# Six layers of two transformer stacks on one core: token halves taken in turn at the borders between phases, turned heads in a score bank, weight steps in quarters

## The reference

```
x = x + 0.5 * swiglu(rms_norm(x, ffn1_norm[l]), ffn1_w13[l], ffn1_w2[l])
h = rms_norm(x, mix_norm[l]);  three attention branches (differential, sliding with sinks, latent)
x = x + jnp.sum(gates * proj, axis=2) @ w_out[l]
x = x + 0.5 * swiglu(rms_norm(x, ffn2_norm[l]), ffn2_w13[l], ffn2_w2[l])
```

```
x = x + 0.5 * rms_norm_2(swiglu_2(rms_norm_2(x, g[0]), ffn_w_in[i, 0], ffn_w_out[i, 0]), g[1])
m = sliding_sink / nsa / moba / sliding_sink attention of rms_norm_2(x, g[2])     (i = 0, 1, 2, 3)
x = x + rms_norm_2(m, g[3])
x = x + 0.5 * rms_norm_2(swiglu_2(rms_norm_2(x, g[4]), ffn_w_in[i, 1], ffn_w_out[i, 1]), g[5])
```

## Time and profile before

| | |
|---|---|
| median of 3 runs | 3773.41 us (3771.87 to 3777.15) |
| the profiled execution | 3778.8 us, span 3777.0 us |
| PE busy | 3436.2 us, 91% of the span |
| PEld, DVE, ACT, POOL busy | 78%, 58%, 48%, 2% |
| mean granted TensorE clock | 0.926 of full speed |
| HBM | 615.62 MB read, 166 GB/s over the span |

### The profile page before, as it was taken

One profiled execution on the slowest core, in us unless ns is written; L12 is line 12 of the kernel. 1 busy time (PEld: TensorE's weight loads), 2 busy tenths in 40 slices (PEclk: granted clock), 3 DMA queues, 4 the chain that ended last, 5 costly groups with the idle time before them and its releaser, 6 DMA issues.

```text
span 3777.0 us, 49507 instructions
## 1 busy us (share of the span) xinstructions
PE 3436.2 (91%) x18184; PEld 2940.8 (78%) x18184; DVE 2186.5 (58%) x2330; ACT 1803.9 (48%) x2261; POOL 92.5 (2%) x208
## 2 busy tenths in 40 slices
PE   7987899999779899998899998789999989998799
PEld 6876677878677788787787877678787978787687
DVE  5565465555655555556555565555656655556555
ACT  4454444444554454445444453344445544444444
POOL 0000000000000000000000000100000000000000
PEclk9987899999878999998999996679999999999899
DMA  6653345545433455454354543235454444454254
GB/s 236 218 188 112 109 169 181 181 178 189 145 106 120 153 189 189 176 180 148 142 179 177 189 167 123 72 106 189 178 191 178 161 150 178 176 191 168 100 200 167
DMA packets 105050, 618.45 MB, mean 164 GB/s; under 512 B 10816, under 2 KB 19008, under 8 KB 34656
## 3 DMA queue, kind: packets, MB, share of 16 engines
q1 hardware_dynamic: 84288, 562.07, 41.4%
q10 hardware_dynamic: 20640, 54.71, 4.3%
HBM read 615.62 MB, written 9.50 MB: 166 GB/s over the span
## 4 chain that ended last, share of the span: by engine, by line
PE 83%; DVE 7%; ACT 4%; issue 3%; DVEq 1%; POOL 1%; DMA 0%; ACTq 0%; POOLq 0%
PE ps L1520 32%; PE ps L1524 16%; PE ps L1584 6%; PE ps L1583 6%; PE ps L1585 6%; PE ps L1541 2%; PE ps L1542 2%; PE ps L1543 2%; PE ps L1559 2%; PE ps L1683 1%; PE ps L1672 1%; DVE wlo L985 1%; ACT v L633 1%; PE ps L1697 1%; PE ps L1698 1%
## 5 line engine op out<-in xcount | busy, mean ns | idle before, releaser
L1520 PE MATMUL ps<-xhl,whi 128*128 128x512 f32 x4944 | 1734.7, 401 | 34.8 <-DVEq L401 34.8
L985 DVE TENSOR_TENSOR wlo<-raw,whi 128x2048 fp32r<-128x2048 f32 x526 | 1204.1, 2292 | 784.4 <-ACT whi L597 784.3
L1524 PE MATMUL ps<-xhl,wlo 128*128 128x256 f32 x4944 | 1289.6, 281 | 0.0
L597 ACT CAST whi<-raw 128x2048 fp32r<-128x2048 f32 x526 | 999.8, 1904 | 226.5 <-PE ps L1585 128.0
L1520 PEld LDWEIGHTS ps<-xhl,whi 128*128 128x128 f32 x4944 | 905.4, 190 | 217.2 <-issue 41.8
L1524 PEld LDWEIGHTS ps<-xhl,wlo 128*128 128x128 f32 x4944 | 946.6, 191 | 55.4
L1584 PE MATMUL ps<-wlo,ht 128*128 128x512 f32 x1056 | 417.2, 395 | 0.0
L1583 PE MATMUL ps<-whi,ht 128*128 128x512 f32 x1056 | 417.1, 395 | 0.0
L1585 PE MATMUL ps<-whi,ht 128*128 128x512 f32 x1056 | 416.6, 395 | 0.0
L670 ACT COPY tg<-ps 128x512 f32<-128x512 f32 x132 | 77.5, 587 | 430.9 <-PE ps L1520 430.9
L1585 PEld LDWEIGHTS ps<-whi,ht 128*128 128x128 f32 x1056 | 198.3, 188 | 48.1
(11 more groups left out here) (242 smaller groups left out, 3718.1 us busy)
## 6 DMA issues: line engine op xcount, KB each, us to landing
raw<-stream SPq DMA_DIRECT2D x528, 1024.0 KB, 4.8
bias<-rel_bias ACTq DMA_DIRECT2D x80, 256.0 KB, 2.7
gain<-gains ACTq DMA_DIRECT2D x19, 1024.0 KB, 4.7
bias<-fixed_bias ACTq DMA_DIRECT2D x40, 256.0 KB, 2.6
rel_bias<-rel_vectors SPq DMA_DIRECT2D x16, 512.0 KB
x<-x_tokens ACTq DMA_DIRECT2D x1, 1024.0 KB, 4.8
y_tokens<-x ACTq DMA_DIRECT2D x1, 1024.0 KB, 3.9
cst<-constants ACTq DMA_DIRECT2D x1, 670.0 KB, 6.6
```

The costliest lines, as they stand in the source:

```text
L597: nc.scalar.copy(whi[:, slot, :], raw[:, slot, :]).then_inc(sem["hi_ready"], 1)
L985: nc.vector.tensor_tensor(wlo[:, slot, :], raw[:, slot, :], whi[:, slot, :].bitcast(F32), ALU.subtract).then_inc(sem["lo_ready"], 1)
L1520: wide = lambda: pe.matmul(ps[:, bank, 0:2 * half], hi[:, k, col0:col0 + P], src[:, k0 + k, :], start=first and k == 0, stop=last and k == ...
L1524: e = pe.matmul(ps[:, bank, 0:half], lo[:, k, col0:col0 + P], src[:, k0 + k, 0:half], start=False, stop=False)
```

## The change

Borders: the whole chain of a between runs for token half 0 and then for half 1, on ScalarE, GpSimd and VectorE, and the splits of the next phase's steps 1 and 2, which stood behind it, are put inside it. PE has no between any more: the next phase turns a half itself (`arrive`), waits for its low parts (`arrived`, new semaphore `x_low`) and multiplies half 0 of its first two steps, turning half 1 in the middle. For that these products are token-major (96 matmuls of 256 columns in an ffn in place of 32 of 512 and 32 of 256). In an ffn the first pair's SwiGLU is then taken token-major by halves and turned by four PE transposes into bank 6. In a projection with such a lead, v comes first; the stream of weights is laid out in that order. gqa2's first group needs both halves at once. At the end of an ffn the last two down steps are done for half 0 and then for half 1; in the plain output projection (`wout`) the last two steps as well.

Weaves: turned heads go to the score bank of the next slot in place of bank 3; the values no longer wait for their low parts, the scores of the next slot do. `brw` has four buffers for two. Product steps are issued in quarters, the tables name how many per slot: gqa2 2, 2, eleven times 1, four times 2, 1, 0; moba twelve times 3, six times 2, 0. Groups of moba come as v, q, k for q, k, v.

```diff
@@ slots
-GQA_SLOTS = {0: [(2, 0)], 1: [(2, 1)], 2: [(3, 0)], 4: [(3, 1)], 5: [(4, 0)], 7: [(4, 1)], 9: [(5, 0)],
...
+GQA_SLOTS = slots_of([part for j in range(2, 8) for part in quarters(j)],
+                     [2, 2] + [1] * 11 + [2, 2, 2, 2, 1, 0])
+MOBA_SLOTS = slots_of([part for j in range(3, 15) for part in quarters(j)],
+                      [3] * 12 + [2] * 6 + [0])
@@ plan, second stack: order of the groups
-        project(f("q", 0, 2), f("k", 0, 2), t("v", 0, 512, 4, 2, 1))
+        project(t("v", 0, 512, 4, 2, 1), f("q", 0, 2), f("k", 0, 2))
...
-            project(f("k", 0, 1), t("v", 0, 256, 8, 1, 1), f("k", 4, 1), t("v", 256, 256, 8, 1, 1),
-                    t("gate", 0, 48, 8, 1, 1))
+            project(f("k", 0, 1), f("k", 4, 1), t("gate", 0, 48, 8, 1, 1))
...
-            by_four = [g for n in range(4) for g in f("q", 4 * n, 1) + f("k", 4 * n, 1) + t("v", 256 * n, 256, 8, 1, 1)]
+            by_four = [g for n in range(4) for g in t("v", 256 * n, 256, 8, 1, 1) + f("q", 4 * n, 1) + f("k", 4 * n, 1)]
@@ ScalarE, ffn and weave
+                def first_pair(tt):
+
+                    if tt == 0:
+                        act.wait_ge(sem["ag_made"], base(ph, "ag_made") + 1)
+                    else:
+                        multiplied(ph.step + 1)
+                    nc.scalar.activation(silu[:, tt, :], ps[:, 4 + tt, 0:T], ACT.Silu).then_inc(sem["silu_first"], 1)
...
+                first_pair(0)
                 split(ph.step + 3)
+                first_pair(1)
+                act.wait_ge(sem["tposed"], base(ph, "tposed") + 1)
+                nc.scalar.copy(ht[:, 0, :, 0, :], ps[:, 6, :].rearrange("p (k t) -> p k t", k=2))\
+                    .then_inc(sem["hi_made"], 1)
...
-                def turned(k):
+                def turned(k, bank):
                     act.wait_ge(sem["tposed"], B["tposed"] + k + 1)
-                    if k >= 4:
-
-                        multiplied(ph.step + n_g + k // 2 - 2)
-                    nc.scalar.copy(brw[:, k // 2 % 2, k % 2, 0:T], ps[:, 3, T:2 * T]).then_inc(sem["hi_made"], 1)
@@ VectorE, between
+                step = after_of(ph).step
+                if ph.gains == 0:
+
+                    dve.wait_ge(sem["vec_stored"], 16)
+                if ph.after == "post":
+                    gained(0)
+                added(0)
+                if ph.final:
+                    final_norm(0)
+                normed(0)
+                if ph.after == "post":
+                    gained(1)
+                else:
+                    added(1)
                 if ph.gains == 0:
                     split(0)
+                low_parts_of(0)
+                if ph.after == "post":
+                    added(1)
+                if ph.final:
+                    final_norm(1)
+                split(step + 1)
+                normed(1)
+                low_parts_of(1)
+                split(step + 2)
@@ TensorE: arrival of a token half, ffn, project, weave
+            def arrive(ph, tt):
+
+                last = before_of(ph)
+                pe.wait_ge(sem["xn_ready"], base(last, "xn_ready") + tt + 1)
+                for half in range(2):
+                    n, k0 = 2 * tt + half, 4 * half
                     for k in range(4):
                         e = pe.transpose(ps[:, n, k * P:(k + 1) * P], o[:, tt, (k0 + k) * P:(k0 + k + 1) * P], ident)
                     e.then_inc(sem["tposed"], 1)
+
+            def arrived(ph, tt):
+
+                last = before_of(ph)
+                pe.wait_ge(sem["x_low"], base(last, "x_low") + 2 * tt + 2)
+
+            def token_cols(dst, w, col0, width, src, tt, ks=range(KD), k0=0, first=0, last=KD - 1):
+
+                hi, lo = (part[:, :, col0:col0 + width] for part in w)
+                for k in ks:
+                    xh = src[:, k0 + k, tt * P:(tt + 1) * P]
+                    xl = src[:, k0 + k, T + tt * P:T + (tt + 1) * P]
+                    pe.matmul(dst, xh, hi[:, k, :], start=k0 + k == first, stop=False)
+                    pe.matmul(dst, xh, lo[:, k, :], start=False, stop=False)
+                    e = pe.matmul(dst, xl, hi[:, k, :], start=False, stop=k0 + k == last)
...
+                def first_pair(tt, turn_between):
+
+                    for part in range(2):
+                        use(ph.step + part)
+                        w = step_parts(ph.step + part, KD, 2 * P)
+                        dst = ps[:, 4 + tt, part * T:(part + 1) * T]
+                        token_cols(dst, w, 0, 2 * P, xhl, tt, range(KD // 2))
+                        if turn_between and part == 1:
+                            arrive(ph, 1)
+                        e = token_cols(dst, w, 0, 2 * P, xhl, tt, range(KD // 2, KD))
+                        if tt == 1:
+                            e.then_inc(sem["step_used"], 1)
+                    if tt == 0:
+                        e.then_inc(sem["ag_made"], 1)
+
+                arrive(ph, 0)
+                arrived(ph, 0)
+                first_pair(0, True)
+                arrived(ph, 1)
+                first_pair(1, False)
+                use(ph.step + 2)
+                w = step_parts(ph.step + 2, KD, 2 * P)
+                feature_tile(0, w, 0, xhl)
+                for tt in range(TT):
+                    pe.wait_ge(sem["h_first"], base(ph, "h_first") + tt + 1)
+                    for kk in range(2):
+                        e = pe.transpose(ps[:, 6, kk * T + tt * P:kk * T + (tt + 1) * P],
+                                         h[:, tt, kk * P:(kk + 1) * P], ident)
+                e.then_inc(sem["tposed"], 1)
+                feature_tile(1, w, P, xhl).then_inc(sem["step_used"], 1)
+                pe.wait_ge(sem["ht_first"], base(ph, "ht_first") + 1)
+                down(ph.step + 3, first=True)
+                up(ph.step + 4, 2)
                 with pe.Fori(2, PAIRS - 1) as j:
                     body(j, ph.step - 1, j)
...
+                for tt in range(TT):
+                    for i in range(2):
+                        c = end - 2 + i
+                        if tt == 0:
+                            pe.wait_ge(sem["ht_ready"], base(ph, "ht_ready") + last - 1 + i)
+                            use(c)
+                        w = step_parts(c, 2, D)
+                        for kk in range(2):
+                            e = rows_by(w, i, tt, kk, False, i == 1)
+                        if tt == 1:
+                            e.then_inc(sem["step_used"], 1)
+                    if tt == 0:
+                        e.then_inc(sem["acc_half"], 1)
...
+                    k = weave_turn(t - 1)
+                    if k is not None:
+
+                        pe.wait_ge(sem["lo_made"], B["lo_made"] + k + 1)
...
-                def turn_heads(k):
+                def turn_heads(k, bank):
                     pe.wait_ge(sem["o_done"], B["o_done"] + 2 * k + 2)
+                    pe.wait_ge(sem["biased"], B["biased"] + min(2 * k + 4, ph.n))
                     for tt in range(TT):
-                        e = pe.transpose(ps[:, 3, T + tt * P:T + (tt + 1) * P], o[:, tt, k * P:(k + 1) * P], ident)
+                        e = pe.transpose(ps[:, bank, tt * P:(tt + 1) * P], o[:, tt, k * P:(k + 1) * P], ident)
                     e.then_inc(sem["tposed"], 1)
 
...
+                arrive(ph, 0)
+                if ph.groups[0].dest != "v":
+                    arrive(ph, 1)
+                    arrived(ph, 1)
+                arrived(ph, 0)
+                for quarter in range(4 * ph.early):
+                    if ph.groups[0].dest == "v" and quarter == 1:
+                        arrive(ph, 1)
+                    if quarter == 2:
+                        arrived(ph, 1)
+                    product(quarter // 4, quarter % 4)
                 for t in range(ph.n + 3):
...
-                    if here:
-                        part_of(*here[0])
+                        turn_heads(k, (t + 1) % 2)
+                    first = (len(here) + 1) // 2
+                    for part in here[:first]:
+                        part_of(*part)
                     if 1 <= t <= ph.n:
                         turn_probs(t - 1)
-                    if len(here) > 1:
-                        part_of(*here[1])
+                    for part in here[first:]:
+                        part_of(*part)
                     if 2 <= t <= ph.n + 1:
@@ TensorE, wout
-                for i in range(4):
+                for i, tt in ((0, 0), (0, 1), (1, 0), (1, 1), (2, 0), (3, 0), (2, 1), (3, 1)):
```

402 lines of the change are left out of this document (220 added, 182 removed), and 3 rows, old and new, of the table MOBA_SLOTS.

## The result

The changed kernel takes 3783.41 us (median of 20 runs, 3771.66 to 3789.90), the kernel before on the same chip 3774.84 (20 runs): ratio 1.0028, 95% interval 1.0021 to 1.0036. I had forecast 3750.5 us, faster; it is 8.6 us slower by the medians, 10.6 by the ratio. The profiled executions differ by 4.4 us (span 3781.4 against 3777.0).

A forecast was written before the change was run, and what follows sets the result against it. TensorE's work plus its standing, mostly at borders, was taken to bound the kernel. Terms 15.8 + 12.2 - 11.9 - 1.2 + 20 - 12 = 22.9 us, off a median of 3773.41, gave 3750.5 us; range 3728 to 3778.

The forecast's parts named there:

- What bounds it: Whole kernel: TensorE's work plus its standing still; the largest wait, 94.8 us, is for normed tokens at the borders.
- plain borders: Borders behind a phase without output norm: both first steps done at 16.1 us, gain 3.2 us behind an FFN.
- the end of an FFN: Last two down steps, now by token halves: TensorE stands about 1.2 us for `ht` in each of 12 FFNs.
- Post borders behind FFNs: Borders behind FFNs with normed output, into FFNs: both first steps done at 19.8 us, gain 1.9 us at three.
- Behind weaves and the final norm: Borders into FFNs there: gain 0.6 us at each of three behind weaves, 3.8 us at the final norm.
- clock* rival: Every border, moba and gqa2: products fall into the half clock, 37.6 us lost, 3788 us; chance 0.12.
- Borders before gqa2: Both borders into gqa2: its first group needs both halves, so nothing covers half 1; loss 4.8 us, twice.
- The first attention's stop: Layers 0 and 1 of the first stack: attention waits for the last k, 10.1 us for 5.16 now.
- covered by the gate step alone: NSA: second k's low parts, 9.3 us behind its matmuls, are covered only by about 5.6 us: -3.7.
- Gain 10 us, twice: Both gqa2 weaves: quarters give every slot product, leaving 4 us of stops; 10 us gained in each.
- nothing from the quarters: Rival for gqa2's weaves: VectorE's queue sets the slots, the 20 us go, 3770.5 us; chance 0.15.
- 5.3 + 3 x 4.6: moba's weave: scores wait for k's emptying, 5.3 us once and 4.6 three times; new stops 19.2 us, loss 12.

The follow-up runs named there:

- e5: Changed kernel with moba's groups v first once, then k, q, v, plus spare TensorE work filling stops before FFNs: 3743.13 us, ratio 0.9918 to the kernel before.
- e7: Changed kernel with moba's groups v first once, then k, q, v, plus another VectorE and ScalarE order at borders before gqa2: 3750.30 us, ratio 0.9930.
- e1: Changed kernel with moba's groups back in the order q, k, v: 3758.77 us, ratio 0.9960 to the kernel before.
- e3: Changed kernel with the old slot tables (half products) in both weaves, new bank and group order kept: 3777.20 us, ratio 1.0006 to the kernel before.
- e8: Changed kernel with moba v first once, then k, q, v, plus VectorE's weight split in gqa2 cut to 128 of 2048 columns: 3730.54 us, ratio 0.9890.
- e10: Changed kernel with turned heads in bank 3 again, quarters and group order kept: 3787.18 us, ratio 1.0026 to the kernel before.
- e4: Changed kernel with everything inside the weaves as before (slots, bank, moba's q, k, v), borders new: 3767.03 us, ratio 0.9978 to the kernel before.
- e13: Changed kernel with moba v first once, then k, q, v, plus ScalarE's weight split in gqa2 cut to 128 of 2048 columns: 3746.48 us, ratio 0.9925.
- e14: Changed kernel with moba v first once, then k, q, v, plus VectorE's emptying and weight split later in all weaves' slots: 3744.79 us, ratio 0.9925.
- e6: Changed kernel with moba v first once, then k, q, v, plus the last two down steps of each FFN mixed: 3756.38 us, ratio 0.9950.

## Why the prediction was wrong, by its steps

- **What bounds it, plain borders, the end of an FFN: right.** Both steps are done 15.86 us after E (forecast 16.1), the gain is 3.3 us (3.2), and the stop is 1.03 us (1.2) in each FFN. The product there ran at a granted clock of 1.00 from its start; before, it was 0.88 over the same work.
- **Post borders behind FFNs: right in the mark.** Done at 20.05 us (19.8), though some 4 us of the product run at half clock, which is more than my 0.3 us of slack has room for; e5 shows that most of it was covered. Behind weaves and the final norm: mechanism right, sizes off. Done at 23.5 and 24.5 us, where I had 22.0 and 20.6 (the 26.2 of before less 3.8, 0.55 and 1.2), and 5.2 to 5.8 us of the product run at half clock. The *clock* rival named this for every border; it came at the post ones and the final norm alone, and its sign, a mean clock below 0.926, did not come (0.931). Removing it in e5 returned 0.9 us behind an FFN and 1.4 to 1.8 behind a weave, as much as the weave borders missed (1.5); at the final norm e5 didn't remove it, and that miss of 3.9 us stays open.
- **Borders before gqa2: right.** First products at 14.4 and 13.8 us (13.7), the first scores 5.5 and 3.1 us later than before (4.8 forecast for each), and e7 took 3 us of the loss back with the order I had blamed. The first attention's stop is 10.03 us (10.1).
- **NSA, the second k "covered by the gate step alone": not settled.** 285.1 us is 2.3 us better than forecast, but the same code took 284.9 to 285.3 us in eight of the profiled executions and 287.8 to 288.9 in four (e1, e3, e7, e8), and the one of before took 288.0.
- **"Gain 10 us, twice" from the quarters: failed.** The step was: every slot has product, so stops in slots without any go. e3 shows 0 for the quarters, e10 and e4 0.4 to 0.6 us for all that changed inside. Product was not what the stops lacked. A stop ends where VectorE and ScalarE are behind, and e8, e13 and e14 show for four of them with what: the split ahead of the heads' outputs (4.4 us), the emptying of q ahead of bias and `brw` (3.9). I had left 4 us of stops; 12.4 stand, besides the 2.7 before the first scores. Against the kernel before, 0.7 us of standing is gone in the first body. I had written this down as a rival, "nothing from the quarters", with 0.15, and had its row, the 3.1 us for `brw` behind an emptied group.
- **moba, "5.3 + 3 x 4.6": mechanism right, size off.** 24.8 us for 19.2: the exponentials and the probabilities' copy stand ahead of the emptying on ScalarE (1.4 us), the wait for their bias ahead of these. And 44 us between the first product and E ran at half clock, before some 17; busy time grew by 4.5 us, and I had allowed 2. The loss was 18.8 us for my 12, in the middle between that and the upper bound of 25.
- **In sum:** borders 8.3 us under the kernel before (e4), weaves 19 over that (ratios 0.9978 and 1.0028), nearly all of it in moba. The recorded chances had 0.13 on slower. The rival "nothing from the quarters" (3770.5) with moba's measured 6.8 us more gives 3777; the rest is that the two kernels differ by 10.6 us by the ratio and by 4.4 in the profiled executions.

What stays open: which of its two lengths gqa2 takes, and why; where those parts of e3's 8 us and e8's 20 lie that their traces don't show; why the plain border of e6 lost 1.0 us; and what the weight split beside GpSimd's step costs at the borders into FFNs, since no run moves it there.

## What to carry to other kernels

Before spreading an engine's work over slots, ask which engine ends each stop and what stands ahead of the awaited instruction in its queue; product in the gap helps only where nothing else is late. An order that is right at one place (v first, so that half 1 is covered at the border) can be wrong in every later round of the same loop: change it for the first round alone. A stop at the consumer is the whole chain between two engines, not the two longest instructions in it.
